# Attention scores: the low queries' products as 64-row matmul pairs, and one reciprocal for two tiles

## What is computed

```python
def attend(qblk):
    sc = jnp.einsum('bqkgd,bskd->bkgqs', qblk, k).astype(jnp.float32) * scale
    p = jax.nn.softmax(sc, axis=-1).astype(v.dtype)
    return jnp.einsum('bkgqs,bskd->bqkgd', p, v)
```

## Time and profile before

| what | us |
|---|---|
| median of three runs | 2303.51 |
| the profiled execution's own time | 2303.42 |
| its span in the profile | 2301.7 |
| TensorE busy (matmul) | 2267.3 |
| VectorE busy | 1077.5 |
| ScalarE busy | 888.7 |
| GpSimd busy | 274.1 |

### The profile page before, as it was taken

How to read it: one execution, slowest core, us unless ns; L and a number is a source line. 1 busy time by engine, 2 the same in 40 slices (tenths; PEclk the granted TensorE clock), 3 DMA queues, 4 the chain that set the end, 5 groups by cost and what they waited for, 6 DMA issues and landing times.

```text
span 2301.7 us, 28551 instructions
## 1 busy us (share of the span) xinstructions
PE 2267.3 (99%) x11640; PEld 1919.2 (83%) x11640; DVE 1077.5 (47%) x1439; ACT 888.7 (39%) x1426; POOL 274.1 (12%) x276
## 2 busy tenths in 40 slices
PE   8999999999999999999999999999999999999998
PEld 7887799988888779998788898887888888888887
DVE  4313399954433259983624252335334344342343
ACT  5222477744322257773434152323222222222232
POOL 0097200000029600000013020000000000000000
PEclk9999999999999999999999999999999999999999
DMA  6111000043311000003421101222111111124232
GB/s 202 37 55 37 1 1 1 1 138 116 90 53 56 19 1 1 1 9 121 147 60 37 64 19 37 100 94 90 39 55 55 36 55 50 41 101 146 92 128 73
DMA packets 104210, 141.48 MB, mean 61 GB/s; under 512 B 11670, under 2 KB 65094, under 8 KB 104102
## 3 DMA queue, kind: packets, MB, share of 16 engines
q1 hardware_dynamic: 104102, 139.97, 18.4%
HBM read 123.18 MB, written 16.78 MB: 61 GB/s over the span
## 4 chain that ended last, share of the span: by engine, by line
PE 95%; DVE 3%; ACT 1%; issue 1%; DMA 0%; DVEq 0%; SPq 0%; ACTq 0%
PE ps L199 24%; PE ps L201 24%; PE ps L200 24%; PE ps L983 5%; PE ps L998 3%; PE ps L999 3%; PE ps L970 2%; PE ps L971 2%; PE ps L947 1%; PE ps L275 1%; PE ps L228 1%; PE ps L934 1%; PE ps L1962 1%; PE ps L684 1%; PE ps L1971 1%
## 5 line engine op out<-in xcount | busy, mean ns | idle before, releaser
L199 PE MATMUL ps<-w_hi,hT_hi 128*128 128x512 f32 (+1 forms) x1760 | 678.5, 386 | 2.4 <-DVE hT_lo L238 1.4
L201 PE MATMUL ps<-w_hi,hT_lo 128*128 128x512 f32 (+1 forms) x1760 | 671.9, 382 | 0.0
L200 PE MATMUL ps<-w_lo,hT_hi 128*128 128x512 f32 (+1 forms) x1760 | 671.5, 382 | 0.0
L183 DVE TENSOR_TENSOR w_lo<-w_raw,w_hi 128x2048 fp32r<-128x2048 f32 x89 | 207.7, 2334 | 539.9 <-ACT w_hi L167 537.3
L199 PEld LDWEIGHTS ps<-w_hi,hT_hi 128*128 128x128 f32 x1760 | 331.2, 188 | 66.9 <-issue 2.1
L201 PEld LDWEIGHTS ps<-w_hi,hT_lo 128*128 128x128 f32 x1760 | 331.0, 188 | 64.5
L200 PEld LDWEIGHTS ps<-w_lo,hT_hi 128*128 128x128 f32 x1760 | 331.4, 188 | 62.5 <-issue 0.5
L167 ACT ACTIVATE w_hi<-w_raw 128x2048 fp32r<-128x2048 f32 x71 | 135.9, 1914 | 504.4 <-PE ps L201 504.4
L199 PE MATMUL ps<-hT_hi,w_hi 128*128 128x512 f32 x832 | 324.1, 390 | 2.1 <-DVE hT_lo L290 1.7
L201 PE MATMUL ps<-hT_hi,w_lo 128*128 128x512 f32 x832 | 323.7, 389 | 0.0
L200 PE MATMUL ps<-hT_lo,w_hi 128*128 128x512 f32 x832 | 323.7, 389 | 0.0
(11 more groups left out here) (203 smaller groups left out, 2363.9 us busy)
## 6 DMA issues: line engine op xcount, KB each, us to landing
w_raw<-in_ffn_w_up SPq DMA_DIRECT2D x44, 512.0 KB, 5.0
w_raw<-in_ffn_w_down SPq DMA_DIRECT2D x22, 1024.0 KB, 5.0
w_raw<-in_w_in SPq DMA_DIRECT2D x21, 1024.0 KB, 5.1
x_mid<-X SPq DMA_DIRECT2D x24, 512.0 KB, 2.9
w_raw<-in_gla_w_in SPq DMA_DIRECT2D x12, 1024.0 KB, 5.2
X<-in_x SPq DMA_DIRECT2D x16, 512.0 KB, 7.0
w_raw<-in_w_out SPq DMA_DIRECT2D x8, 1024.0 KB, 6.7
X<-x_mid SPq DMA_DIRECT2D x16, 512.0 KB, 7.5
```

The source lines that it names most:

```text
L183: engine.tensor_tensor(self.p.w_lo[:, slot, 0:size], self.p.w_raw[:, slot, 0:size], plane(self.p.w_hi[:, slot, 0:size]), ALU.subtract).the ...
L199: nc.tensor.matmul(out, a_hi, b_hi, start=first, stop=False)
L200: nc.tensor.matmul(out, a_hi, b_lo, start=False, stop=False)
L201: return nc.tensor.matmul(out, a_lo, b_hi, start=False, stop=last)
```

## The change

The tile's scores now are three products for each half of the keys: `QT_hi` with `KT_st` as before (high x high and high x low; 128 rows), and low queries with high keys alone, as a contraction over 64 rows. Low x low is left out. The first 512 keys' `K_hi` lies on partitions 0 to 63 (in `KT_st`), the last 512 keys' `K_hi` on partitions 64 to 127 (in the new `KT_up`), so the two low matmuls of a tile use different halves of the array's rows and different PSUM banks. The even step issues: the high part of n, the low pair of n, then a wait until tile n-1 has its exponentials, and the low pair of n+1, which starts that tile's accumulation; the odd step issues only that tile's high part, which closes it. `KT_up` takes the room of `KT_hi` (first keys' `K_hi` for the subtraction now stands for a while in the still unused second half of `QT_hi`). VectorE takes two tiles' reciprocals in one instruction in odd steps.

```diff
@@ class Attention
-        self.KT_hi = prog.at("KT_hi", [P, SEQ], kb + 88, F32R)
+        self.KT_up = prog.at("KT_up", [P, KV, SEQ // 2], kb + 88, F32R)
...
+    def low_keys(self, i):
+
+        return self.KT_up[HD:P, i // 2, :] if i % 2 else self.QT_hi[HD:P, 1, 0:SEQ // 2]
@@ pe
-        def scores(n):
+        def high_scores(n):
             head, t = n // TT, n % TT
             if t == 0:
                 pe.wait_ge(self.lo_done, 2 * (KV + head) + 2)
                 pe.wait_ge(self.k_top, 2 * KV)
+            if n % 2 == 0:
+                if n >= 2:
+                    pe.wait_ge(self.exp_done, n - 1)
+                else:
+                    self.gates(pe, 2)
+            for half in range(2):
+                mm = nc.tensor.matmul(prog.ps[:, 2 * (n % 2) + half, :],
+                                      self.QT_hi[:, head % 2, t * P:(t + 1) * P],
+                                      self.KT_st[:, head // (H_B // KV), half * 512:(half + 1) * 512],
+                                      start=(n % 2 == 0), stop=(n % 2 == 1))
+            return mm
+
+        def low_scores(n, first):
+            head, t = n // TT, n % TT
+            g, tok = head // (H_B // KV), slice(t * P, (t + 1) * P)
+            nc.tensor.matmul(prog.ps[:, 2 * (n % 2), :], self.QT_lo[0:HD, head % 2, tok],
+                             self.KT_st[0:HD, g, 0:512], start=first, stop=not first)
+            return nc.tensor.matmul(prog.ps[:, 2 * (n % 2) + 1, :], self.QT_lo[HD:P, head % 2, tok],
+                                    self.KT_up[HD:P, g, :], start=first, stop=not first)
+
+        def scores(n):
+            mm = high_scores(n)
+            if n % 2 == 1:
+                mm.then_inc(self.s_ready, 1)
+                return
+            low_scores(n, False).then_inc(self.s_ready, 1)
             if n >= 2:
-                pe.wait_ge(self.exp_done, n - 1)
+                pe.wait_ge(self.exp_done, n)
             else:
-                self.gates(pe, 2 * n + 2)
-            for half in range(2):
-                keys = self.KT_st[:, head // (H_B // KV), half * 512:(half + 1) * 512]
-                out = prog.ps[:, 2 * (n % 2) + half, :]
-                nc.tensor.matmul(out, self.QT_hi[:, head % 2, t * P:(t + 1) * P], keys, start=True, stop=False)
-                mm = nc.tensor.matmul(out, self.QT_lo[:, head % 2, t * P:(t + 1) * P], keys, start=False, stop=True)
-            mm.then_inc(self.s_ready, 1)
+                self.gates(pe, 4)
+            low_scores(n + 1, True)
@@ dve
-                nc.vector.reciprocal(self.inv[:, m:m + 1], self.sm[:, m:m + 1]).then_inc(self.inv_done, 1)
+                if m % 2 == 1:
+                    nc.vector.reciprocal(self.inv[:, m - 1:m + 1], self.sm[:, m - 1:m + 1]).then_inc(self.inv_done, 2)
```

More of the change, by code:

```diff
@@ L1040, in act_first @@
                 act.wait_ge(self.lo_done, i - 1)
-            nc.scalar.activation(self.KT_hi[HD:P, cols], prog.ps[HD:P, self.turn_bank(i), :], ACT.Copy
+            nc.scalar.activation(self.low_keys(i), prog.ps[HD:P, self.turn_bank(i), :], ACT.Copy
                                  ).then_inc(self.hi_done, 1)
@@ L1117, in dve_first @@
                                     prog.ps[HD:P, self.turn_bank(i), :],
-                                    plane(self.KT_hi[HD:P, i % 2 * 512:(i % 2 + 1) * 512]), ALU.subtract
+                                    plane(self.low_keys(i)), ALU.subtract
                                     ).then_inc(self.lo_done, 1)
```

## The result

The changed kernel takes 2317.84 us, the median of 6 runs (2316.68 to 2319.10), against 2305.46 (2303.42 to 2306.13) for the kernel before on the same chips: ratio 1.0056, 95% interval 1.0043 to 1.0068. It is slower by 12.4 us. The forecast was +11.2 us on a base of 2303.42. The profiled execution took 2318.34 us, its span is 2316.6.

What follows compares the result with a forecast made beforehand. TensorE was taken as the bound, with VectorE only 0.29 us a tile behind. Plain pairs -1.1 us and turning pairs +12.3 us gave +11.2 us on 2303.42, thus 2314.6 us; range 2291 to 2326.

Steps and rivals of the forecast that it cites:

- Price of a change of height: TensorE switching between full-height and 64-row matmuls, twice a pair of tiles: 0.19 us each, 0.09 late plus 0.10 exposed load.
- block of four: The four 64-row score matmuls of a pair of tiles: 0.90 us, against 0.93 for the full-height ones replaced.
- plain pairs: Tile pairs with no head's queries turned between: TensorE still decides, -0.03 us each, times 36 = -1.1 us.
- turning pair: Tile pair with a head's queries turned between: 7.08 us against 6.64, +0.44 times 28 = +12.3 us.
- the new wait (W): Odd tile's low part waits for tile n-1's exponentials, one tile fresher; TensorE stands about 0.7 us in turning pairs.
- The starts of the layers: First pairs of each layer wait a little longer for fresh exponentials; stands under 1 us, left to the range.
- The clock: TensorE's granted clock in attention stays at 1.00, the 2.4 GHz level.
- The reciprocal: One reciprocal per pair less on VectorE, 0.15 us: counted 0; at most 9.6 us if VectorE became the bound.
- A: Score matmuls: height changes cost nothing and halves start together; net -11.2, 2292.2 us. Chance 0.22.
- B: Height changes cost 0.09, next weights load under the drain; block 0.70 us, net +1, 2304.6 us. Chance 0.16.
- C: Score matmul halves do not run side by side; block 1.31 us, total 2334.7 us. Chance 0.10.
- D: Four 64-row score matmuls in a row, 0.93 us, height changes free; total 2315.8 us. Chance 0.05.

Runs made afterwards that it cites:

- e10: The changed kernel with only turn_o moved behind the value products: 2316.09 us, ratio 1.0042 to the kernel before.
- e11: The changed kernel with only the odd tile's maximum taken ahead of QT_lo on VectorE: 2329.34 us, ratio 1.0101 to the kernel before.
- e5: The changed kernel with the odd tile's maximum ahead of QT_lo and turn_o behind the value products: 2305.28 us, ratio 0.9999 to the kernel before.
- e4: The kernel before with only the reciprocals taken once for two tiles: 2305.08 us, ratio 1.0001 to the kernel before.
- e3: The changed kernel with both halves' low matmuls on partitions 0 to 63: 2347.46 us, ratio 1.0184 to the kernel before.
- e1_full: The changed kernel with the low products on all 128 rows, so no row pairs: 2322.51 us, ratio 1.0075 to the kernel before.

## Why the prediction was right

**The base and the block.** Price of a change of height: forecast 0.09 late and 0.10 for an exposed load, there and back. Measured: the load 0.32 us behind the last start, in both directions, as forecast. On the way there it is exposed for 0.10, as forecast (the starts at 383.05 and 383.38 are 0.33 apart instead of 0.23), on the way back, which the forecast priced the same without a row for it, only for 0.06 (the transposes take 1.09 instead of 1.03). The offset between the halves, forecast 0.05, is 0.00 to 0.01; both halves' loads run at once. So the block of four took 0.82 us, not 0.90. Against that the odd tile's transposes now take 0.94 for 0.87, which I had not priced. The two cancel: 5.95 - 0.93 + 0.82 + 0.07 = 5.91 for plain pairs, measured 5.92, forecast 5.92. That agreement is luck.

**The turning pair.** Forecast 7.08, measured 7.00. The size and the place were right; the cause was named only by half. The forecast way over the new wait (W) exists: second low pair 383.38, transposes 383.71, `PT_hi` 384.46, exponentials 385.43, `QT_hi` 386.52, `QT_lo` 387.16, maximum 387.77, exponentials 389.02, second low pair 390.36, which is 6.98 us. (The forecast's 7.08 had 0.47 from the low pair to the transposes, which is 0.33, and 0.70 from there to `PT_hi`, which is 0.75.) But beside it runs a loop through `turn_o` (O): from the transposes 0.75, 0.97, 1.09 and 0.64 to `QT_lo`, 0.84 to `turn_o` at 388.00, 1.46 to the high part at 389.46, 1.25 to the transposes at 390.71, 7.00 us. This loop set the turning pair already before the change, and the rows were there to show it: the earlier trace rows give 0.70, 0.97, 1.09, 0.64 and 0.84, and behind `turn_o` at 380.68 come the values and four score matmuls, to the next even transposes, which start at 383.08 in the timeline of the kernel before (the chain has them at 383.24):

```profile
383.08 1.03 PE L983 MATMUL ps<-ident,PR 128*128 128x128 f32 x8
```

That is 2.40 more, in all 6.64. I took the stand at `turn_o` for a fixed 0.22 us that the new wait would swallow. In truth the change puts both tiles' low parts behind `turn_o` and ahead of the transposes: 1.46 + 1.25 = 2.71 for 2.40 in the loop's TensorE part, and 0.75 for 0.70 to `PT_hi` behind the exposed load, together the 0.36 us by which the pair grew. The odd step, where the change saves 0.47, only has a longer stand. The sign that I had named for the new wait, idle time of the 64-row matmuls of 0.5 to 0.7 us in turning pairs, is absent from the 24 later turning pairs; the waits have it four times, in the first heads. The stand is at `turn_o`:

```profile
PE ps L951 <- DVE QT_lo L1130: 11.2, 24, 0.5
...
PE ps L982 <- ACT PR L1089: 5.1, 4, 2.2
```

Opening O alone gives nothing since W takes over (e10); lengthening the one lengthens the pair (e11); opening W and moving `turn_o` gives 6.70 (e5). The text's claim that the stand at `turn_o` is part of the turning pair's 0.7 us was right, the claim that the change's 0.7 is the new wait's was wrong: in the change O holds the pair and W is 0.02 us behind it. That both come out near the forecast is in part luck.

**The starts of the layers** were forecast as small and in the range. They cost more than I gave them: 4.7 us in the first heads' turning pairs, where the sum had 4 x 0.44 = 1.8, and 1.6 us ahead of the first transposes. Fresh exponentials are a real wait there (PE L982 above, four stands of up to 2.2 us), and the clock comes in, below. In the sum this makes up for the later turning pairs, which grew by 0.36 and not 0.44 us each: 10.6 us forecast for those 24, 8.6 measured. So the nearness of +11.2 and +12.4 is partly luck too.

**The clock** was forecast at 1.00 throughout attention. It was not: some 2.7 us of the profiled execution are its price, which no term of the forecast had; see the last section.

**The reciprocal**, costed at nothing: e4 gives nothing. **The rivals:** A (clean pairs) fails on the price of changing height (the block takes 0.82, where A had 0.47); B on the exposed loads, though the block's 0.82 lies between its 0.70 and my 0.90; C and D on the common starts and on e3.

## What to carry to other kernels

Work moved ahead of a wait is not free because another step got shorter by the same amount: draw the loop that sets the period, from the row that closes it back to itself, and ask on which side of it the moved work lies. When two loops are within a few hundredths, a fix of one shows nothing; try both, and each alone. Row pairs of half height pay only when enough of them share one way there and back: here a lone pair lost 0.11 to 0.13 us, two in a row won 0.11, and the win was smaller than what their place in the order cost.

## What the runs showed of the hardware that I had not expected

**Two cuts of the granted clock at the start of attention.** Windows of the changed kernel, columns as in the earlier trace rows:

```profile
272.00:276.00 4.00, 2.66 (x12) 1.35 (x11) 2.20 (x2) 2.91 (x3) 0.00 (x0) 1.00 0.00 0
276.00:280.00 4.00, 3.68 (x14) 2.38 (x15) 1.99 (x4) 2.80 (x7) 0.00 (x0) 0.57 0.00 0
280.00:286.00 6.00, 3.60 (x23) 2.20 (x21) 5.29 (x9) 4.58 (x9) 0.00 (x0) 1.00 0.00 0
286.00:292.00 6.00, 6.00 (x38) 5.76 (x37) 3.47 (x5) 3.84 (x7) 1.17 (x2) 0.72 0.00 0
292.00:300.00 8.00, 7.57 (x54) 5.72 (x52) 6.92 (x14) 6.26 (x13) 0.00 (x0) 1.00 0.01 2
```

Between 276 and 280 and again between 286 and 292 us the mean granted clock is 0.57 and 0.72, that is, for part of the time the lower of the two levels (1.2 GHz). The timeline of the same stretch shows 64-row matmuls of 0.79 us for 0.39 to 0.50, and eight transposes of 1.77 for 1.03 to 1.09:

```profile
276.32 1.08 PE L973 MATMUL ps<-KT_st,QT_hi 128*128 128x512 f32 x2 [1.66 <-ACT PR L1089]
...
277.33 0.79 PE L982 MATMUL ps<-KT_st,QT_lo 64*128 64x512 f32 x1
...
278.48 1.77 PE L1008 MATMUL ps<-ident,PR 128*128 128x128 f32 x8
...
285.61 0.50 PE L982 MATMUL ps<-KT_st,QT_lo 64*128 64x512 f32 x1 [2.22 <-ACT PR L1089]
```

Ahead of the first cut TensorE had stood about 1.7 us for the exponentials, ahead of the second 2.2 us. The kernel before has the first stand too (1.65 us) and keeps 1.00. The first layer lost 2.7 us more than the second, which had the same order and no cut; that is my figure for the price. Other runs had some in other places: e5_maxfirst at 276 to 280 (0.59), e11_maxonly from 276 to 286 (0.72 and 0.91), e3_samerows at 286 to 292 (0.76), e10_lateo in the second layer (840 to 850: 0.83); e1_full, with the change's order and stands of 1.65 and 1.66 us in the first layer, had none, and is slower than the change all the same. What brings a cut about was not settled: both cuts come behind stands of TensorE, but other stands of the same length had none.

**Loads of weights at half height.** In the timeline of the result the load of L982 at 383.15 runs under the matmul of L982 from 383.05, on the same rows. "TensorE: Matmul & The Clock Gate", Part 3, of the Trainium skill says in its list of what overlaps that such a load goes beside running matmuls only where the row group differs, though the same section also names a background weight buffer. This trace disagrees with the list, at half height as at 96 rows, and is in keeping with the buffer. It agrees with that section's common starts of matmuls on different row groups (0.00 to 0.01 us apart here).
